# Up projections with 512-column products, and a block inverse over four quadrants of the array, in a two-block transformer kernel

## The reference

```python
def conv_ffn(h, w_up, conv_w, conv_b, w_down):
    gu = h @ w_up                       # 1024 -> 2 * 2816
    g, u = gu[..., :D_FF], gu[..., D_FF:]
    g = causal_depthwise_conv(g, conv_w) + conv_b     # width 3
    return (jax.nn.silu(g) * u) @ w_down
def swiglu(x, w13, w2):                 # the other four
    gate, up = jnp.split(x @ w13, 2, axis=-1)
    return (jax.nn.silu(gate) * up) @ w2
```

```python
t_inv = lax.linalg.triangular_solve(lower + eye, jnp.broadcast_to(eye, lower.shape),
                                    left_side=True, lower=True, unit_diagonal=True)
u = t_inv @ vb
w = t_inv @ (kb * jnp.exp(g)[..., None])
```

## Time and profile before

| | us |
|---|---|
| median of 3 runs | 2231.65 (2230.42 to 2234.09) |
| the profiled execution | 2230.76 |
| its span, first to last instruction | 2228.8 |
| PE busy | 2128.3 |
| DVE busy | 1396.4 |
| ACT busy | 1022.0 |

### The profile page before, as it was taken

One profiled execution on the slowest core, in us unless ns is written; L12 is line 12 of the kernel. 1 busy time (PEld: TensorE's weight loads), 2 busy tenths in 40 slices (PEclk: granted clock), 3 DMA queues, 4 the chain that ended last, 5 costly groups with the idle time before them and its releaser, 6 DMA issues.

```text
span 2228.8 us, 37711 instructions
## 1 busy us (share of the span) xinstructions
PE 2128.3 (95%) x16692; PEld 1928.2 (87%) x16692; DVE 1396.4 (63%) x1568; ACT 1022.0 (46%) x1165; POOL 160.3 (7%) x119
## 2 busy tenths in 40 slices
PE   6789999889999999999998999999999999899998
PEld 5778998868998998898778799889979977888996
DVE  8866665475665554684865675465548576667554
ACT  5564543553543443355552344334434564434442
POOL 1000000000000100241000020020004300002000
PEclk9899999989999999999999999999999999999999
DMA  7145555513555665564421465556556633125653
GB/s 186 29 142 156 178 184 170 178 57 95 189 189 172 192 190 175 161 224 155 133 77 40 151 194 185 180 171 212 180 165 199 199 115 113 59 94 164 198 179 123
DMA packets 259498, 342.68 MB, mean 154 GB/s; under 512 B 23335, under 2 KB 169421, under 8 KB 259335
## 3 DMA queue, kind: packets, MB, share of 16 engines
q1 hardware_dynamic: 253968, 329.95, 46.2%
q0 software_dynamic: 2768, 9.08, 1.3%
q10 hardware_dynamic: 2599, 1.23, 0.4%
HBM read 338.14 MB, written 2.10 MB: 153 GB/s over the span
## 4 chain that ended last, share of the span: by engine, by line
PE 84%; DVE 9%; ACT 3%; DMA 2%; issue 1%; POOL 0%; ACTq 0%; DVEq 0%; POOLq 0%
PE acc L1797 20%; PE acc L1799 20%; PE acc L1798 20%; PE acc L1813 3%; PE trp L1797 2%; DVE w_lo L1122 2%; PE trp L1799 2%; PE trp L1798 2%; PE acc L2296 2%; PE acc L2291 2%; PE acc L1820 1%; PE acc L1862 1%; DMA raw<-in_w_in 1%; ACT w_hi L668 1%; PE trp L2296 1%
## 5 line engine op out<-in xcount | busy, mean ns | idle before, releaser
L1122 DVE TENSOR_TENSOR w_lo<-raw,w_hi 128x2048 fp32r<-128x2048 f32 (+1 forms) x316 | 730.0, 2312 | 474.4 <-ACT w_hi L668 473.1
L668 ACT ACTIVATE w_hi<-raw 128x2048 fp32r<-128x2048 f32 (+1 forms) x316 | 594.0, 1880 | 620.7 <-PE acc L1799 280.8
L1797 PE MATMUL acc<-xT_hi,w_hi 128*128 128x256 f32 x2496 | 708.3, 284 | 3.5 <-DVE w_lo L1122 3.5
L1798 PE MATMUL acc<-xT_lo,w_hi 128*128 128x256 f32 x2496 | 707.3, 283 | 0.0
L1799 PE MATMUL acc<-xT_hi,w_lo 128*128 128x256 f32 x2496 | 707.2, 283 | 0.0
L1797 PEld LDWEIGHTS acc<-xT_hi,w_hi 128*128 128x128 f32 x2496 | 480.1, 192 | 4.8 <-issue 3.5
L1798 PEld LDWEIGHTS acc<-xT_lo,w_hi 128*128 128x128 f32 x2496 | 480.1, 192 | 0.1
L1799 PEld LDWEIGHTS acc<-xT_hi,w_lo 128*128 128x128 f32 x2496 | 480.1, 192 | 0.0
L1799 PE MATMUL acc<-w_hi,hT_lo 128*128 128x512 f32 x528 | 209.3, 396 | 0.0
L1797 PE MATMUL acc<-w_hi,hT_hi 128*128 128x512 f32 x528 | 209.3, 396 | 0.0
L1798 PE MATMUL acc<-w_lo,hT_hi 128*128 128x512 f32 x528 | 209.3, 396 | 0.0
(11 more groups left out here) (369 smaller groups left out, 2700.5 us busy)
## 6 DMA issues: line engine op xcount, KB each, us to landing
raw<-in_ffn_w SPq DMA_DIRECT2D x184, 512.0 KB
raw<-in_w_in SPq DMA_DIRECT2D x60, 1024.0 KB
raw<-in_ffn_w_up SPq DMA_DIRECT2D x88, 512.0 KB
raw<-in_ffn_w SPq DMA_DIRECT2D x40, 1024.0 KB
raw<-in_ffn_w_down SPq DMA_DIRECT2D x20, 1024.0 KB
raw<-in_ssm_w_glu SPq DMA_DIRECT2D x16, 512.0 KB
raw<-in_kv_w SPq DMA_DIRECT2D x8, 1024.0 KB
raw<-in_w_branch_a SPq DMA_DIRECT2D x8, 1024.0 KB
```

Source lines behind the costliest of these rows:

```text
L668: A(w_hi[:, p % SPL, 0:kt, :], raw[:, p % RAW, 0:kt, :], ACT.Copy).then_inc(hi_ready, 1)
L1122: V_.tensor_tensor(w_lo[:, p % SPL, 0:kt, :], raw[:, p % RAW, 0:kt, :], w_hi[:, p % SPL, 0:kt, :].bitcast(F32), ALU.subtract).then_inc(lo_ ...
L1797: mm(out, ah, bh, start=first, stop=False, skip_group_check=True)
L1798: mm(out, ah, bl, start=False, stop=False, skip_group_check=True)
```

## The change

**Up projections.** The two parts of the activations now lie side by side in one tensor, `xT[:, k, 0:2, :]`. In columns 1 to 9 of each FFN (`MERGED`), `merged` replaces `features`: one matmul of 512 columns multiplies `w_hi` with both parts, and one of 256 columns adds `w_lo` times the hi part. The results of hi*hi + lo*hi and of hi*lo then lie in separate halves of a bank, so a column needs four banks. Odd columns use the four banks of `trp`, even ones use both accumulators. ACT copies the second halves into a new buffer `folds` (two copies of 512 elements), DVE adds the first halves (two additions of 512 elements), and the chain of the column goes on from `folds`.

**Inverse.** Ys and W of a chunk now lie on the other side of the partitions than U. So X U uses the off-diagonal quadrants, W Y also the off-diagonal ones, and the transpose of Z the diagonal ones, and the two kinds are written alternately. The start of W is made after U instead of before, in four instructions of 64 partitions instead of two of 128.

```diff
+            def merged(name, j):
+                u = place(name, j)
+                if u is None:
+                    if turns.index((name, j)):
+                        pe.wait_ge(sem("turn_freed"), turns.index((name, j)))
+                else:
+                    claim(u)
+                    claim(u + 1)
+                out = bank_parts(name, j)
+                for i, p in enumerate(gemms[name][j]):
+                    pe.wait_ge(lo_ready, p + 1)
+                    _, _, k0, kt, _ = panels[p]
+                    for n in range(4):
+                        c, tile = slice(n * P, n * P + P), out[n // 2][:, n % 2]
+                        for k in range(kt):
+                            mm(tile, w_hi[:, p % SPL, k, c], xT[:, k0 + k], start=i == k == 0, stop=False, skip_group_check=True)
+                            ins = mm(tile[:, 0], w_lo[:, p % SPL, k, c], xT_hi[:, k0 + k, :], start=False,
+                                     stop=i == len(gemms[name][j]) - 1 and k == kt - 1, skip_group_check=True)
+                    ins.then_inc(panel_used, 1)
...
 # ScalarE, gate(j, u)
+                    if j in MERGED:
+                        act.wait_ge(panel_used, gemms[f"up{f}"][j][-1] + 1)
+                        for half, v in enumerate(bank_parts(f"up{f}", j)):
+                            A(folds[:, j % 2, 2 * half:2 * half + 2], v[:, :, 1], ACT.Copy).then_inc(sem("fold_copied"), 1)
+                        act.wait_ge(sem("gate_folded"), folded_no(f, j))
...
 # VectorE, gate(j, u)
+                    if j in MERGED:
+                        n, (gs, us) = folded_no(f, j), bank_parts(f"up{f}", j)
+                        dve.wait_ge(sem("fold_copied"), 2 * n - 1)
+                        V_.tensor_tensor(g, g, gs[:, :, 0], ALU.add).then_inc(sem("gate_folded"), 1)
+                        dve.wait_ge(sem("fold_copied"), 2 * n)
+                        ins = V_.tensor_tensor(up, up, us[:, :, 0], ALU.add)
...
 # VectorE, start of the inverse
-                for t in range(TT):
-                    dve.wait_ge(sem(f"X_ready{t}"), 3 * i + 1)
-                    step(V_.tensor_tensor(UT[:, t, 1], bc(const(C_SID, BL), 1, DH), Xs[0][:, t, 0], ALU.subtract))
-                step.settle()
                 for t in range(TT):
                     dve.wait_ge(sem(f"Y_filled{t}"), 7 * i + 1)
                     V_.tensor_tensor(UT[:, t, 0], bc(const(C_SID, BL), 1, DH), small_bank(trp[t]), ALU.subtract).then_inc(sem(f"U_started{t}"), 1)
+                for t in range(TT):
+                    dve.wait_ge(sem(f"X_ready{t}"), 3 * i + 1)
+                    for b in range(2):
+                        V_.tensor_tensor(UT[side(1 - b), t, 1], bc(cst[side(b), C_SID:C_SID + BL], 1, DH), Xs[0][side(b), t, 0],
+                                         ALU.subtract).then_inc(sem(f"W_started{t}"), 1)
...
 # TensorE, the levels of the inverse
-                                q = side(b)
-                                ins = tile(small_bank(trp[t])[q, h], Xs[lv // 2][q, t, lv % 2, h, :], UT[q, t, 0, h, :] if lv else ident[q, q])
+                                q, o = side(b), side(1 - b if lv else b)
+                                ins = tile(small_bank(trp[t])[o, h], Xs[lv // 2][q, t, lv % 2, h, :], UT[q, t, 0, h, :] if lv else ident[q, q])
...
                         for h in range(DH):
                             for b in range(2):
-                                q = side(b)
-                                tile(Z2(u)[q, 0, h], UT[q, t, 1, h, :], Ys[q, t, h, :])
-                        for h in range(DH):
-                            for b in range(2 if lv < SMALL - 1 else 1):
-                                q = side(b)
-                                ins = tile(Z2(u)[q, 1, h], Ys[q, t, h, :], UT[q, t, 1, h, :])
+                                q, o = side(b), side(1 - b)
+                                ins = tile(Z2(u)[q, 0, h], UT[o, t, 1, h, :], Ys[o, t, h, :])
+                                if b == 0 or lv < SMALL - 1:
+                                    ins = tile(Z2(u)[o, 1, h], Ys[o, t, h, :], UT[o, t, 1, h, :])
```

128 lines of the change are left out of this document (89 added, 39 removed).

## The result

| | before | after |
|---|---|---|
| median of the runs, us | 2231.03 (4 runs) | 2212.53 (4 runs) |
| ratio, with its 95% interval | | 0.9922 (0.9899 to 0.9946) |
| the profiled execution, us | 2230.76 | 2210.96 |
| its span, us | 2228.8 | 2208.8 |
| PE, DVE, ACT busy, us | 2128.3, 1396.4, 1022.0 | 2098.4, 1462.1, 1082.6 |

What follows compares the result with a forecast made beforehand. PE's own pace was taken to bound the up projections, and PE taking turns with DVE and ACT the inverse. Terms -23.0 + 0 - 12.0 = -35.0 us from 2230.76 gave 2195.8, as median 2196.7; range 2189 to 2213.

Steps and rivals of the forecast that it cites:

- Merged products: Up projections on PE: 1728 products at 346.7 ns instead of 360, -23.0 us, bounds 0 and -23.
- The merged matmul reads `xT` and the same weight slots, so I take 226.7: Up projections: the 512-column matmul gets the branch product's 226.7 ns, not the down projection's 235.
- ACT and DVE: Merged columns: the added copies and additions stay hidden behind PE, 0 us; upper bound 37 us if all in series.
- The round of 11.3 us against a column of 11.1: FFNs with convolution: DVE's work per merged column exceeds PE's column, falling back 0.2 us each, 1.8 over nine.
- the cover of 1.8 us: Merged columns with convolution: the split ends 9.3 us after the column, and PE wants the panel at 11.1.
- The inverse: Block inverse, two layers: four quadrants side by side save 6.0 us per layer, -12.0 us; bounds -18.7 and +0.6.
- the walk through the levels: Inverse, per layer: 0.7 us saved in level 1, 1.4 each in levels 2 to 4, 1.1 in level 5; sum 6.0.
- The 1.3 us per layer kept for the clock: Inverse: shorter bursts may lower the granted clock; doubling its loss costs 1.3 us per layer, kept for the range.
- A: Rival, up projections: 512-column matmuls run at 235 to 240 ns, -8.6 to 0 us, so 2211 to 2220; chance 0.11.
- B: Rival, inverse: the quadrants don't overlap four at a time, +0.6 instead of -12 us, so 2209; chance 0.13.
- C: Rival, two FFNs with convolution: DVE gets round too late, 2208 us, up to 2233 in full series; chance 0.08.
- D: Rival, merged products: the `w_lo` load isn't hidden behind the 512-column matmul, 2525 us in full; chance 0.04.

Runs made afterwards that it cites:

- e14: The changed kernel with 32 bytes left unused ahead of the hidden units' tensor: 2210.39 us.
- e18: The changed kernel with one extra 12-column matmul in each FFN and 160 unused bytes ahead of the hidden units: 2193.55 us, ratio to before 0.9826.
- e13: The changed kernel with one extra 12-column matmul in each FFN, ahead of the third product of the first merged column: 2207.28 us, ratio 0.9886.

## Why the prediction was wrong

**Merged products, forecast -23.0, measured -13.3.** The direction, the place and DVE's and ACT's part were right; the term was mis-sized. The step that failed is "The merged matmul reads `xT` and the same weight slots, so I take 226.7". The prediction saw that the two paces of the earlier trace rows go with the tensor. It took the tensor for the cause, where it is the place of the stationary operand (`e14` to `e18`), and it took a pace found in a stream of equal matmuls for one of two sizes in turn. There each product is 353.3 ns or 346.7, by which rhythm the stream has fallen into, though its operands begin at the same place within 256 bytes. The forecast 346.7 is the fast one to the tenth (`e13`, and one FFN of six, by the moment at which one `w_lo` ended), which is no merit of the sum: it knew of no second rhythm. 1728 x 6.3 = 10.9 us lie between the FFNs' means of 353.4 and 347.1; the changed kernel got 1.8 of these.

**ACT and DVE, forecast 0, measured 0.** PE waits on `w_lo` in no merged column, in either kind of FFN. The round of 11.3 us against a column of 11.1 was right. That nothing shows of it is owed to the slower products, as the column is 11.31; where they are fast, the cover of 1.8 us is just used up in the ninth column and costs 0.15 to 0.18 us and that column's rhythm (`e13`).

**The inverse, forecast -12.0, measured -6.1.** Four quadrants do work side by side. The first Z begins 1156.23, 1156.24, 1156.24, 1156.25 us, and its 32 tiles take 0.94 us as forecast. Their weight loads begin 6 or 7 ns apart and last 129. The rule of the Trainium skill (page "TensorE: Matmul & The Clock Gate", on packing, "The mechanism"), by which a load overlaps only when the row group differs, does not hold here: two of these four share their rows. The step that failed is the walk through the levels: it let PE's shorter work arrive up to DVE's subtractions, 1.4 us in each of levels 2 to 4 and 1.1 in level 5, and knew of no third limit. The runs show two. One is the instruction supply, with pauses of 6.4 us against 2.2, so 4.2 of the missing 5.9; the two longest fall into levels 3 to 4, which brought 0.6 and -0.3 us instead of 1.4. The other is the clock. In the two stretches it is at its lower level for 6.3 and 6.5 us instead of 2.2 and 4.0, which by half of the difference is up to 2.1 and 1.2 us (an estimate from these four numbers), and the end from the join to the product takes 0.9 and 0.3 us more. Both together are enough for what is missing. The shares come from the traces; no run takes one of the two limits away alone. The 1.3 us per layer kept for the clock was of the right order here, and far too small for the inverse alone, whose first layer spends 16.9 us at the lower clock and takes 42.3 us, 0.8 more than before.

**The rivals.** A came closest in time (2211 to 2220) and named the right quantity, 235 instead of 226.7; its reason, the row of the down projection, was the wrong one. That the time lies in A's span, and at the very end of the range of 2189 to 2213, is luck in part: A had the products at -8.6 us and the inverse at its full -12, where they were -13.3 and -6.1. B did not happen. C did not happen. D did not happen: a load of `w_lo` fits beside each long matmul.

**What stays open.** Why these streams have two rhythms, why a `w_lo` that ends at one moment turns one into the other, and why a place within 256 bytes changes a pace by 7 ns, is not shown; `e18` matches the weights' and the input's place, and whether the absolute or the relative one counts wasn't tried. Nor was it tried to keep TensorE's supply up in the inverse, for instance with fewer and larger tiles. Why the clock falls early in some executions and not in others stays open too.

## What to carry to other kernels

Where the path is a stream of matmuls back to back, a distance of starts taken from another stream carries an error of some 3% (226.8 against 234.2 ns here): read it from a stream with the same sequence of shapes, and look at whether it repeats with a period, which says that something is out of step. Try the beginning of the stationary tensor at the same place within 256 bytes as the moving one: 160 unused bytes and six small matmuls brought as much here as the whole change. Where tiles are small, count instructions per us as well as columns, and expect the granted clock to take a part of what shorter work gives.

## What the runs showed of the hardware that I had not expected

- One stream of alternating 512- and 256-column matmuls has two stable rhythms, 353.3 and 346.7 ns per pair. A 12-column matmul at the right point turns the slow one into the fast one (17 of 18 FFNs then kept it over most columns), and so did a next panel that was ready 23 to 48 ns before the last matmul of the present one (9 of 9, against none of 7 at 52 to 67 ns).
- A stream of 512-column matmuls goes at 226.8, 232.3, 233.3 or 234.2 ns according to where its stationary operand begins within 256 bytes (128, 0, 32, 224).
- Instructions come to TensorE in packets of 256, in the inverse no closer than 3.7 us and nowhere in the two programs closer than 3.3. It stopped at their seams where small tiles asked for 69 a us (2.2 us in all) or for twice that (6.4 us).
- 64x64 tiles on all four quadrants of the array, rows and columns shared, start four matmuls in 58 ns. A float32 tile is two of them, so 32 tiles take 0.94 us, where two quadrants do 16.
- With four quadrants instead of two, the clock fell to its lower level ahead of the join in 28 of 34 layers, in 15 of them ahead of level 5 already; with two in none of 4.
